# Gelu and weights for two slots at a time, and one more group of query weights kept, in a decoder trunk on one core

## What is computed

```python
q = einsum('td,de->te', xt, w_pq).reshape(T, 8, 2, 128)      # w_pq is 1024 x 2048
s = einsum('thcd,hcnd->thcn', q, sub_keys)                   # top 16 of 128, twice, then top 16 of 256 sums
u = take(u_tab, ids, axis=0)                                 # 128 rows of 1024 for each token
a = gelu(einsum('cd,chkd->chk', xc, u))
vv = take(v_tab, ids, axis=0)
out = einsum('chk,chkd->cd', gates * a, vv)
```

## Time and profile before

| what | value |
|---|---|
| median of 3 runs | 1786.49 us |
| profiled execution, its own time | 1784.41 us |
| its span | 1782.7 us |
| mean granted clock of PE, share of full speed | 0.853 |
| HBM read | 621.53 MB |
| gathers (software_dynamic queue) | 536.94 MB, 78.8% of 16 engines' span |
| weights and the rest (hardware_dynamic queue) | 85.71 MB, 12.9% |
| mean rate over the span | 349 GB/s |

### The profile page before, as it was taken

The page is one execution under the profiler, slowest core; times in us unless marked ns, Lnnn a source line. Parts: engine busy times, 40 slices in busy tenths (PEclk is TensorE's granted clock), DMA queues, the critical chain, the costliest instruction groups (busy, mean ns, idle before and its releaser), DMA issues.

```text
span 1782.7 us, 15641 instructions
## 1 busy us (share of the span) xinstructions
PE 1290.3 (72%) x4541; PEld 717.6 (40%) x4568; DVE 1111.1 (62%) x2405; ACT 514.7 (29%) x1398; POOL 1018.7 (57%) x1061
## 2 busy tenths in 40 slices
PE   8987675676774887877865698977877467666654
PEld 6555342342431545533342264634444134222221
DVE  3356777638487547645467848755549758755455
ACT  3322234313222312343222332354222212322221
POOL 2026666645566454665656655566656656666664
PEclk9999887888887999978988799988988788777776
DMA  9349999998999899998998999998998989999997
GB/s 356 107 165 360 364 388 376 359 345 323 394 399 368 298 347 354 407 383 304 418 412 307 355 372 412 409 384 317 364 418 332 358 312 341 339 372 374 351 353 296
DMA packets 186333, 623.57 MB, mean 350 GB/s; under 512 B 25600, under 2 KB 25600, under 8 KB 186256
## 3 DMA queue, kind: packets, MB, share of 16 engines
q0 software_dynamic: 147456, 536.94, 78.8%
q1 hardware_dynamic: 38800, 85.71, 12.9%
HBM read 621.53 MB, written 1.05 MB: 349 GB/s over the span
## 4 chain that ended last, share of the span: by engine, by line
PE 36%; DVE 23%; issue 18%; another core or an unknown queue 9%; DMA 7%; POOL 3%; ACT 3%; SPq 0%; DVEq 0%; ACTq 0%; PEldq 0%; POOLq 0%
PE acc L1650 19%; DVE u_ring L840 11%; PE pair L1503 4%; PE pair L1575 4%; DVE h L850 4%; PE pair L1490 3%; DMA u_ring<-in_peer_u,ids 3%; POOL v_ring L553 2%; POOL u_ring L539 2%; DMA wbuf<-in_fox_w_q 1%; DVE scratch L704 1%; DMA wbuf<-in_peer_w_q 1%; PE pair L1532 1%; ACT L1221 1%
## 5 line engine op out<-in xcount | busy, mean ns | idle before, releaser
L1650 PE MATMUL acc<-v_ring,diag 128*128 128x512 f32 x1524 | 801.4, 684 | 387.7 <-issue 186.0
L553 POOL DMA_INDIRECT v_ring<-in_peer_v,ids x512 | 507.3, 991 | 477.9 <-PE acc L1650 283.2
L840 DVE SCALAR_TENSOR_TENSOR u_ring<-u_ring,pair 128x1024 f32<-128x1024 f32 x508 | 599.6, 1217 | 212.6 <-DMA u_ring<-in_peer_u,ids 175.2
L1650 PEld LDWEIGHTS acc<-v_ring,diag 128*128 128x128 f32 x1524 | 327.5, 222 | 810.5 <-issue 749.9
L539 POOL DMA_INDIRECT u_ring<-in_peer_u,ids x512 | 498.4, 973 | 270.3 <-issue 246.4
L1221 ACT ACTIVATE gelus<-dots 128x4 f32<-128x4 f32 x128 | 26.4, 207 | 653.1 <-DVE u_ring L840 431.5
L850 DVE SCALAR_TENSOR_TENSOR h<-v_ring,weights_s,h 128x1024 f32<-128x1024 f32 x128 | 164.4, 1284 | 19.0 <-issue 7.0
L1575 PE MATMUL pair<-xT,wbuf 128*128 128x128 f32 x896 | 112.1, 281 | 30.1 <-issue 15.2
L1234 ACT ACTIVATE diag<-ident,weights_s 128x128 f32<-128x128 f32 x381 | 125.5, 391 | 10.9 <-issue 4.2
L1575 PEld LDWEIGHTS pair<-xT,wbuf 128*128 128x128 f32 x896 | 107.4, 196 | 34.5 <-issue 20.3
L1221 ACT ACT_TABLE_LOAD x56 | 71.8, 1283 | 169.6 <-DVE u_ring L840 150.8
(11 more groups left out here) (199 smaller groups left out, 1042.0 us busy)
## 6 DMA issues: line engine op xcount, KB each, us to landing
wbuf<-in_peer_w_q SPq DMA_DIRECT2D x24, 1024.0 KB
wbuf<-in_kv_w SPq DMA_DIRECT2D x10, 1024.0 KB
u_ring<-in_peer_u,ids POOLq DMA_INDIRECT x512
v_ring<-in_peer_v,ids POOLq DMA_INDIRECT x512
wbuf<-in_fox_w_q SPq DMA_DIRECT2D x8, 1024.0 KB
wbuf<-in_fox_w_o SPq DMA_DIRECT2D x8, 1024.0 KB
wbuf<-in_gla_w_o SPq DMA_DIRECT2D x7, 1024.0 KB
wbuf<-in_gla_w_in SPq DMA_DIRECT2D x6, 1024.0 KB
```

The lines of the kernel that those rows point to most:

```text
L553: pool.indirect_dma_start(v_ring[:, j, :], None, v_rows, bass.IndirectOffsetOnAxis(ap=ids[:, b, at:at + 1], axis=0)).then_inc(v_loaded[j], 16)
L840: nc.vector.scalar_tensor_tensor(out=u_ring[:, j, :], in0=u_ring[:, j, :], scalar=1.0, in1=near, op0=ALU.mult, op1=ALU.mult, accum_out=dot ...
L1650: ins = nc.tensor.matmul(acc[:, i, :], diag[:, k, :], v_ring[:, j, i * HALF:(i + 1) * HALF], start=False, stop=False)
```

## The change

ACT's half is cut into two pairs of slots (`TWO = 2`, `TWOS = 4` a round): Gelu, the two weights and the diagonals of a pair follow when its two dots are done. `dots_free` and `gelu_ready` now count four a round. DVE looks at `dots_free` before each pair; before the h updates it waits for the second pair's `gelu_ready`. ACT's wait for `vec_free` in half 0 moves ahead of the first Gelu.

Of the weights: blocks 6 and 7 of the query weights of layer 0 (group 3) stay from tile 0 to tile 1 in places 2 and 3, as 2 and 3 (group 1) did in places 0 and 1. Tile 1 of layer 0 therefore takes its groups in the order 1, 3, 0, 2, and only groups 0 and 2 are loaded again. GLA's output projection for tile 1, which had places 2 and 3 in turn, goes into `late[0]`, `late[1]`, `vtok` and `qkT`, once GLA's own products of tile 1 are done (`full(("o", 1))`).

```diff
+TWO = 2
+TWOS = RING // TWO
...
+SPARE = NARROW + 1
...
+GROUPS = {(layer, b): (0, 1, 2, 3) for layer in range(2) for b in range(TILES)}
+GROUPS[0, 1] = (1, 3, 0, 2)
+
+KEPT_BLOCKS = {(("pq", 0, 1), i): (("pq", 0, 0), i) for i in (2, 3, 6, 7)}
...
     def route(layer, b, j):
-        for i in (2 * j, 2 * j + 1):
+        g = GROUPS[layer, b][j]
+        for i in (2 * g, 2 * g + 1):
...
+              (("pq", 0, 0), 6): 2, (("pq", 0, 0), 7): 3, (("wo", 0, 1), 0): LATE, (("wo", 0, 1), 1): LATE + 1,
+              (("wo", 0, 1), 2): SPARE, (("wo", 0, 1), 3): SPARE + 1,
...
-    gla_done = (("wo", 0, 1), 0)
-    last = {LATE: (0, gla_done), LATE + 1: (0, gla_done)}
+    last = {place: (0, GLA_DONE) for place in (LATE, LATE + 1, SPARE, SPARE + 1)}
...
                     place, _, before = PLACE_OF[key]
-                    if before:
+                    if before == GLA_DONE:
+                        sp.wait_ge(*full(("o", 1)))
+                    elif before:
                         sp.wait_ge(*multiplied(before))
...
-                dve.wait_ge(dots_free, r * (RING // SUB) + (q + 1))
                 for j in range(q * SUB, (q + 1) * SUB):
+                    if j % TWO == 0:
+                        dve.wait_ge(dots_free, r * TWOS + (j // TWO + 1))
                     dve.wait_ge(u_loaded[j], r * 16 + 16)
...
-                    dve.wait_ge(gelu_ready, r * (RING // SUB) + 1)
+                    dve.wait_ge(gelu_ready, r * TWOS + TWOS // 2)
...
-                s = slice(q * SUB, (q + 1) * SUB)
-                act.wait_ge(u_free, r * RING + (RING + (q + 1) * SUB))
-                nc.scalar.activation(gelus[:, s], dots[:, s], ACT.Gelu).then_inc(dots_free, 1)
-                act.wait_ge(dots_free, r * (RING // SUB) + (RING // SUB + q + 1))
                 if q == 0:
                     act.wait_ge(vec_free, r * VEC + VEC)
...
+                for t in range(q * SUB // TWO, (q + 1) * SUB // TWO):
+                    slots = range(t * TWO, (t + 1) * TWO)
+                    s = slice(t * TWO, (t + 1) * TWO)
+                    act.wait_ge(u_free, r * RING + (RING + (t + 1) * TWO))
+                    nc.scalar.activation(gelus[:, s], dots[:, s], ACT.Gelu).then_inc(dots_free, 1)
+                    act.wait_ge(dots_free, r * TWOS + (TWOS + t + 1))
+                    for j in slots:
...
+                    ins.then_inc(gelu_ready, 1)
+                    act.wait_ge(gelu_ready, r * TWOS + (t + 1))
+                    for k, j in enumerate(PE_SLOTS):
+                        if j in slots and not is_last(r, j):
```

More of the change, by code:

```diff
@@ L125, in weight_releases @@
                          ((("pq", 0, 0), 4), [("v", 2), ("v", 3)] + [("r", i) for i in range(4)] + [("k", 0), ("k", 1)]),
-                         ((("fl", 0), 0), [(("pq", 0, 0), 2), (("pq", 0, 0), 3)]),
+                         ((("fl", 0), 0), [(("pq", 0, 0), i) for i in (2, 3, 6, 7)]),
                          ((("V", 1), 0), [(("K", 0), i) for i in range(4)])):
@@ L325, in yoco_kernel @@
         places += [t[:, :, :].rearrange("p c n -> p (c n)") for t in (late[0], late[1], narrow)]
+        places += [vtok[:, :, :].rearrange("p b d -> p (b d)"),
+                   qkT[:, :, :, :, :].rearrange("p b a h t -> p (b a h t)")]
         gain_o = gate_o[:, 1, :]
@@ L345, in yoco_kernel @@
         zeros_ready = sem("zeros_ready")
-        w_loaded = [sem(f"w_loaded{i}") for i in range(NARROW + 1)]
+        w_loaded = [sem(f"w_loaded{i}") for i in range(SPARE + 2)]
         w_used = sem("w_used")
@@ L1218, in half @@
                 layer, b = PHASES[ph]
-                s = slice(q * SUB, (q + 1) * SUB)
-                act.wait_ge(u_free, r * RING + (RING + (q + 1) * SUB))
-                nc.scalar.activation(gelus[:, s], dots[:, s], ACT.Gelu).then_inc(dots_free, 1)
-                act.wait_ge(dots_free, r * (RING // SUB) + (RING // SUB + q + 1))
                 if q == 0:
                     act.wait_ge(vec_free, r * VEC + VEC)
[L1225 to L1235, removed]
+                for t in range(q * SUB // TWO, (q + 1) * SUB // TWO):
[5 more added lines that the diff above has]
+                    for j in slots:
+                        ins = nc.scalar.activation(
+                            weights_s[:, j:j + 1], gelus[:, j:j + 1], ACT.Copy,
+                            scale=gates[:, b, bass.ds(r * RING + (j - ph * SLOTS), 1)])
+                    ins.then_inc(gelu_ready, 1)
+                    act.wait_ge(gelu_ready, r * TWOS + (t + 1))
+                    for k, j in enumerate(PE_SLOTS):
+                        if j in slots and not is_last(r, j):
+                            act.wait_ge(v_free, r * len(PE_SLOTS) + (k + 1))
+                            nc.scalar.activation(diag[:, k, :], ident[:, :], ACT.Copy,
+                                                 scale=weights_s[:, j:j + 1]).then_inc(diag_ready, 1)
@@ L1567, in queries @@
                 x = x_of((f"ffn{layer}", b))
-                kept = (("pq", layer, b), 2 * j) in KEPT_BLOCKS.values()
+                first = 2 * GROUPS[layer, b][j]
+                kept = (("pq", layer, b), first) in KEPT_BLOCKS.values()
                 clear(dst[:, 0, :])
-                for i in (2 * j, 2 * j + 1):
+                for i in (first, first + 1):
                     w = block_of((("pq", layer, b), i)).rearrange("p (c n) -> p c n", n=HALF)
@@ L1576, in queries @@
                                                    x[:, c, :], start=False, stop=(c == KC - 1 and m == 3))
-                    if i != 2 * j:
+                    if i != first:
                         ins.then_inc(queryT_full, 1)
```

12 lines of the change are left out of this document (6 added, 6 removed).

## The result

The changed kernel took 1781.01 us (median of 21 runs), the kernel before on the same chip 1791.91 (21 runs). The ratio is 0.9915, 95% interval 0.9894 to 0.9936: 0.85% faster, 15 us. I had forecast 45 us. The direction is right, the time lies in the range, the size is a third.

The account below looks back on a forecast made before the run. POOL's gather issue was taken as the bound, held by v slots that PE frees late because its bursts start late. 1784.4 − 44 − 1 = 1739, against the median 1741 us; 8-in-10 range 1695 to 1788.

Parts of the forecast that it names:

- Part 1's mechanism: Gelu, weights and diagonals in pairs instead of fours let PE's expert bursts begin 2.7 us earlier.
- Part 1's term, −44: Gain from pairs: earlier PE starts free v slots sooner for POOL; −44 us, ends 0 and −140.
- only these I trust to follow: 0.62 × 140 = 87: Of 140 us (52 rounds × 2.7), only the 62% of POOL's stops that end with PE follow its earlier start: 87 us.
- rival (a): POOL's slot releases are not what they seem; only 23 diagonal-bound PE starts count, a quarter comes through: −16 us, 1770; chance 25%.
- The h updates lose nothing: VectorE's h updates behind the second pair's Gelu: no loss, since the table load is already done; 0 us.
- Up to 217 us are lost: DMA from 150 to 1770 us: 589 MB would take 1403 us at 420 GB/s; too little issued loses up to 217.
- Half of it I expect to be given back: Half of the 87 us is lost again where DMA is full, or u landings or DVE's top-k work come late next.
- Gelu's table load and 128 more Gelus at 0: On ScalarE: table load paid as before; 27 us of added Gelus covered by its waits for dots; 0 us.
- Part 2, −1 (−5 to +5): Weights: two 1 MB blocks not reloaded, output projection's blocks loaded earlier; −1 us, ends −5 and +5.
- Rival (b), 1673: All of PE's earlier start comes through: −87 to −140 us, middle 1673; chance 12%.
- Rival (c): No gain: ACT or DVE eat it, or POOL waits for landings instead; 1786 us, chance 10%.
- Rival (d), slower by the clock: Holes between PE's finer bursts lower its granted clock: +30 us if in 40 of 64 rounds, 1816; chance 8%.

Follow-up runs that it names:

- e7: Changed kernel with PE summing the query products over half of the channels, 16 instead of 32 matmuls a group; 1729.9 us, 0.9698 of the kernel before.
- e13: Kernel before with only Gelu, weights and diagonals in pairs, weight stream and group order as before; 1599.0 us, 0.9726 where the kernel before takes 1645.
- e1: Kernel before with only Gelu, weights and diagonals in pairs, weight stream and group order as before; 1769.6 us, 0.9892 where the kernel before takes 1786.
- e17: Changed kernel with Gelu, weight and diagonal for one slot at a time; 1588.4 us, 0.9651 where the kernel before takes 1645.
- e9: Changed kernel plus up to 24 unneeded transfers of 1 MB on the queue of the weights; 1653.8 us, 1.0056 of the kernel before.
- e12: Changed kernel as it is, against the kernel before on a chip where that takes 1645 us; 1596.0 us, 0.9699.
- e14: Kernel before with only the changes to weight loads, their places and group order, Gelu still in fours; 1638.9 us, 0.9967 where the kernel before takes 1645.
- e2: Kernel before with only the changes to weight loads, their places and group order, Gelu still in fours; 1782.8 us, 0.9965 where the kernel before takes 1786.
- e4: Changed kernel with PE multiplying only 128 of 1024 columns of each expert slot, in one instruction; 1729.6 us, 0.9638 of the kernel before.
- e8: Changed kernel with PE's expert products and VectorE's dots and h updates over 128 of 1024 columns; 1702.9 us, 0.9515 of the kernel before.
- e6: Changed kernel with every half written out in place of the loops of PE, ScalarE and VectorE; 1768.9 us, 0.9900 of the kernel before.
- e16: Kernel before, unedited, run again for its trace where it takes 1645 us; 1645.9 us, 1.0015.

## Why the prediction was wrong in size

- *Part 1's mechanism:* right. PE begins 1.4 us behind the second dot, and its idle time before expert matmuls fell by 52 us.
- *Part 1's term, −44:* **the step that failed is "only these I trust to follow: 0.62 × 140 = 87".** On the chips of the result the term measured 15 to 19 us, 0.11 to 0.14 of the 140 in place of 0.31. The step took all of the 148 us under PE's name as set by PE's late start. Of these, 65 us (19 stops) were; 35 stood behind PE's other work (e7 shows that they go with that work), 24 were unexplained, the rest were stops under 0.6 us. The 55 unexplained us named "remote", the 4.46 us of the earlier trace rows among them, weren't in the 148: these I had given to rival (a). And the rule that what doesn't hang on the start stays as it is failed too: the late starts lost 44 us, but the stops behind PE's other work gained 28. Why they grow on these chips, and not on the others, is open. With 65/239 in place of 0.62 the sum would give 19 us; that this is what was measured may be chance.
- *The same term on the other kind of chip:* 45.7 by e13, 0.33 of the 140, and POOL's waits for PE fall by the third that I had named. The factors came from a trace of the first kind, with 93.5 us of stops that this kind lacks, so the agreement is in part luck. From 150 to 1770 us I had forecast 372 GB/s; on the first kind it is 364 as before.
- *"The h updates lose nothing":* a term at 0 that wasn't 0. The weights of slots 2 and 3 now stand behind two diagonals that wait for PE, and POOL's waits for VectorE's updates rose from 8.9 to 21.7 us; on the second kind from 3.6 to 11.9. The size scatters: e1, pairs alone on the first kind, has 6.0.
- *"Up to 217 us are lost":* too much. The share column of the earlier trace rows says 0.95, while stretches at 420 GB/s show 1.02 to 1.03. By these shares the DMA was idle for about 7% of the 1620 us, an estimate of 113 us; in the rest it was slow. Of the same 147456 gather packets the page's share makes 78.8% x 1782.7 = 1405 us on the first kind of chip and 82.0% x 1644.8 = 1349 on the second. An earlier issue can't win that back.
- *"Half of it I expect to be given back", since the DMA is full in places:* right in kind on the second kind of chip. e17's 5.4 us per us, e9's 57.8 us for 25 MB and the windows of e12 show the ceiling. On the first kind, at 365 GB/s, no run shows it.
- *Gelu's table load and 128 more Gelus at 0:* not contradicted. The diagonals waited 22.4 us in all instead of 10.9, just over the 20 that I had set as a sign of trouble; on the second kind of chip it is 10.4 instead of 7.0.
- *Part 2, −1 (−5 to +5):* 5.8 measured by e14 (3.5 to 7.6), 6 by e2: its end, or just beyond. PE takes the output projection's first block at 405.2 with no wait for a transfer. Which of its edits gives the 6 us wasn't split.
- *Rival (a), 1770:* the outcome. 0.9915 x 1786.5 = 1771. Its reason holds in part: some of the releases are not what the list of waits says. That its sum (a quarter of 62 us) gave the right number is luck, for the late starts alone lost 44 us.
- *Rival (b), 1673:* not seen; on the second kind of chip the DMA's ceiling stands in front of it. *Rival (c):* excluded by the interval.
- *Rival (d), slower by the clock:* no. The granted clock is 0.859 after and 0.853 before, and 0.892 against 0.877 on the second kind of chip. Nor does the pause alone set the price that the earlier trace rows gave: behind a pause of 10.09 us 16 records took 9.77 us, 0.61 each, less than the 0.84 behind 2.93. The rule of the Trainium skill ("TensorE: Matmul & The Clock Gate", "Why this matters for your kernels") to keep gaps between bursts short is not refuted: the gaps before expert bursts got shorter in sum (387.7 to 335.8 us), so by that rule too the clock should rise.

**What stays open.** What makes the unexplained stops on the first kind of chip. It is not PE's work on the slots (e4), nor VectorE's (e8), nor loops (e6). With the work on the slots light the kernel takes 1703 us there, 107 more than the whole changed kernel on the second kind, though a lower clock for PE's other work is in that. The 85 us of stops and the slower packets come and go with the kind, and the slow register operations come only with them; that one of them causes the others was not shown, nor that it is the chip and not its load at the time. Nor was it shown why the stops behind PE's other work grow there with the change.

## What to carry to other kernels

Before a wait is counted as gain, compare each long one with the end of the work that it is put down to; those that end long after it belong to something else and get no share of the term. Of those that remain, count only the ones whose burst began out of idleness; a burst that stands behind other work doesn't start earlier. A run with work left out is read beside its granted clock. Read the DMA's busy share beside its GB/s: a low rate at a full share is a slow transfer that no earlier issue helps. And when a ratio is far from a well-founded term, repeat it on another chip before the theory is changed.

## What the hardware showed that I had not expected

- The same kernel takes 1786 to 1792 us on some chips and 1645 on others (8%), with the runs of the kernel before spread over 1.3% in e1's comparison and over 0.3% in e9's, and the same change is worth 0.9915 and 0.9699.
- With PE's work on the slots cut from 789 to 205 us its mean granted clock fell from 0.859 to 0.656 (e4), and its other work took 24% longer.
- On the first kind 49 of 448 register operations of ScalarE in the changed kernel's trace take about 0.7 us, most others 0.035 to 0.046; in the kernel before 17 of 336, with light work on the slots 126. On the second kind there is none.
- Some of the waits named "issue" and "remote" belong to the slower chips alone: e16 has no "remote" row for v gathers, where the earlier trace rows have 62.5 us.
